# Modulation groups, branch A's keys and branch B's norm sums in a two-layer transformer block: three edits of order and layout

## The reference, cut to what matters

```python
def rms_norm(x, g):
    y = xf * lax.rsqrt(jnp.mean(xf * xf, axis=-1, keepdims=True) + NORM_EPS)
    return (y * g.astype(jnp.float32)).astype(x.dtype)
def modulate(h, shift, scale):
    return h * (1 + scale) + shift
...
mod_lat = (jax.nn.silu(c) @ w_ada[l] + b_ada[l])[:, None, :]
p_l = modulate(rms_norm(x, lp['g_norm1']), sh1, sc1) @ lp['w_in']
...
q, k, v = _split(p, (A_Q_W, A_KV_W, A_KV_W))          # branch A: 512 + 128 + 128 columns
q = rms_norm(q.reshape(b, t, A_HEADS, HEAD_DIM), q_gain)   # keys the same, then both rotated
...
cq, ckv, kr = _split(p, (B_Q_LORA, B_KV_LORA, B_ROPE))  # branch B: 384 + 256 + 32 columns
q = (rms_norm(cq, q_gain) @ w_q_up).reshape(b, t, B_HEADS, B_NOPE + B_ROPE)
kv = (rms_norm(ckv, kv_gain) @ w_kv_up).reshape(b, t, B_HEADS, B_NOPE + B_V)
```

## Time and profile before

| | us |
|---|---|
| median of 3 runs | 2586.5 |
| lowest and highest | 2586.43 and 2590.49 |
| profiled execution: its own time | 2591.72 |
| profiled execution: span of the records | 2589.9 |

### The profile page before, as it was taken

The page is one execution under the profiler, slowest core; times in us unless marked ns, Lnnn a source line. Parts: engine busy times, 40 slices in busy tenths (PEclk is TensorE's granted clock), DMA queues, the critical chain, the costliest instruction groups (busy, mean ns, idle before and its releaser), DMA issues. The chain is left out here.

```text
span 2589.9 us, 46521 instructions
## 1 busy us (share of the span) xinstructions
PE 2490.4 (96%) x20808; PEld 1476.5 (57%) x20808; DVE 805.2 (31%) x1651; ACT 574.8 (22%) x1233; POOL 233.7 (9%) x243
## 2 busy tenths in 40 slices
PE   6999999999999999999999999999999999999998
PEld 4444654455555554444444445556466667687887
DVE  2542333253444432121010002441555554321101
ACT  3353323122223211020000002441332323111100
POOL 0000000122222300000000000010022323000000
PEclk9999999999999999999999999999999899899999
DMA  7102111233232334222222224112122111145443
GB/s 285 50 17 73 42 57 49 90 105 110 67 139 68 132 111 151 73 98 81 74 75 79 73 81 151 49 66 90 41 83 67 51 59 60 61 138 177 154 155 106
DMA packets 64391, 238.81 MB, mean 92 GB/s; under 512 B 7009, under 2 KB 8049, under 8 KB 63425
## 3 DMA queue, kind: packets, MB, share of 16 engines
q1 hardware_dynamic: 61824, 220.23, 25.1%
...
HBM read 234.76 MB, written 1.05 MB: 91 GB/s over the span
## 5 line engine op out<-in xcount | busy, mean ns | idle before, releaser
L420 PE MATMUL psum<-normed,panel_ring 128*128 128x512 f32 (+1 forms) x3136 | 1166.4, 517 | 5.1 <-ACT normed L648 4.1
L420 PEld LDWEIGHTS psum<-normed,panel_ring 128*128 128x128 f32 x3136 | 575.6, 191 | 425.6 <-issue 374.0
L420 PE MATMUL psum<-arena,panel_ring 128*128 128x512 f32 (+1 forms) x1792 | 609.8, 494 | 1.8 <-ACT arena L1067 1.8
L420 PE MATMUL psum<-arena 64*64 64x64 f32 (+5 forms) x12696 | 522.0, 251 | 41.6 <-ACT arena L739 10.3
L420 PEld LDWEIGHTS psum<-arena 64*64 64x64 f32 (+2 forms) x12696 | 343.3, 141 | 334.1 <-issue 214.6
L420 PEld LDWEIGHTS psum<-arena,panel_ring 128*128 128x128 f32 x1792 | 335.2, 191 | 225.7 <-issue 200.3
L714 DVE TENSOR_REDUCE softmax_stats<-psum 128x1 f32<-128x512 f32 (+1 forms) x144 | 83.8, 600 | 178.8 <-PE psum L420 177.7
L739 ACT ACTIVATE arena<-psum,softmax_stats 128x512 f32<-128x512 f32 (+1 forms) x144 | 87.7, 613 | 220.0 <-PE psum L697 111.0
L1819 DVE TENSOR_TENSOR arena<-arena 128x512 f32<-128x512 f32 (+1 forms) x64 | 35.8, 559 | 305.8 <-ACT arena L1806 305.8
L1695 DVE SCALAR_TENSOR_TENSOR arena<-psum,modulation,arena 128x256 f32<-128x256 f32 x24 | 10.9, 480 | 313.9 <-PE psum L420 313.9
L1571 POOL TENSOR_SCALAR arena<-arena 128x64 f32<-128x64 f32 x96 | 72.2, 766 | 323.2 <-DVE arena L1617 178.1
...
## 6 DMA issues: line engine op xcount, KB each, us to landing
panel_ring<-panels SPq DMA_DIRECT2D x398, 512.0 KB, 3.3
arena<-panels SPq DMA_DIRECT2D x16, 512.0 KB, 14.8
...
```

The costliest lines, as they stand in the source:

```text
L420: return nc.tensor.matmul(out, lhsT, rhs, start=start, stop=stop, skip_group_check=check)
```

## The change

1. At the start, the sums of squares on TensorE come behind modulation group 0, and the spread of `stage_scale` comes behind group 1. `ROW3` gets a second bank (6).
2. Branch A projects the keys first. `begin` waits for the keys and the first query tile at group 0 and for one further query tile at each later group of heads.
3. Branch B sums squares with tokens on partitions. GpSimd adds the square tiles of a group (two additions for the queries, one for the keys and values), TensorE turns the result into two columns per 128 tokens, ScalarE takes the root of these few columns, VectorE their reciprocal, TensorE spreads them again, and ScalarE copies the spread tile out of PSUM. The key-value sums come ahead of the sixth panel, and the key part's rotation ahead of the second spread. Nine more steps of B are placed before A's attention: its third panel and the first sums. Bank counts and step counts follow.

```diff
                     e.wait_ge(x_in[k // 4].h, 16)
                 nc.scalar.activation(h[:, k, :], x[:, k, :], ACT.Square).then_inc(squared.h, 1)
             yield
+            yield
 
         def pe(e):
+            yield
             e.wait_ge(added.h, added.at(KT - 2))
             token_sums(bank, acc, T, True)
             e.wait_ge(squared.h, squared.at(KT))
@@ -595,7 +597,8 @@
                     e.wait_ge(added.h, added.at(k - 1))
                 nc.vector.tensor_tensor(acc, h[:, 0, :] if k == 1 else acc, h[:, k, :], ALU.add).then_inc(added.h, 1)
             yield
-        return Stage(name, 1, pe=pe, act=act, dve=dve)
+            yield
+        return Stage(name, 2, pe=pe, act=act, dve=dve)
 
 
     def stage_scale(name, l, tok, bank, sums_full, final=False):
...
         col0 = 0 if l < DEPTH - 1 else CTX
 
         def pe(e):
-            begin(e)
             for s in range(n_items + 3):
                 if s < n_items:
                     g, qt = items[s]
                     t, half, nk = groups[g]
+                    if qt == 0 and half == halves[0][0]:
+                        begin(e, t)
                     if exp_done.at(2 * (s - 1) + 2) > 0:
                         e.wait_ge(exp_done.h, exp_done.at(2 * (s - 1) + 2))
                     for i in range(2):
...
         qw = slice(0, T) if l < DEPTH - 1 else mid
         lat = slice(qw.stop - qw.start - SEQ, qw.stop - qw.start)
         q, k, v, rot, sq, tmp, consts = (at[n] for n in ("a_q", "a_k", "a_v", "a_rot", "a_sq", "a_tmp", "t_consts"))
-        tile = [q[:, j, :] for j in range(4)] + [k]
-        n_of = [qw.stop - qw.start] * 4 + [T]
+        tile = [k] + [q[:, j, :] for j in range(4)]
+        n_of = [T] + [qw.stop - qw.start] * 4
         proj, sums, rots, vb = (Banks("a_" + n, b, t) for n, b, t in
                                 (("proj", [0, 1, 2], 5), ("sums", [3], 5), ("rots", [4], 5), ("values", [5], 1)))
         squared, normed, rotated = sem("a_squared", 5), sem("a_normed", 5), sem("a_rotated", 5)
...
         def pe(e):
             for s in range(7):
                 if s < 5:
-                    for i, _ in enumerate(panel_fm(e, proj, l, P_A + s, h, qw if s < 4 else full_row, ready if s == 0 else None)):
+                    for i, _ in enumerate(panel_fm(e, proj, l, P_A + (s + 4) % 5, h, qw if s else full_row, ready if s == 0 else None)):
                         if i < 7:
                             yield
                 if s == 5:
...
                     e.wait_ge(sums.free.h, sums.free.at(j + 1))
                     r = tmp[:, j % 2, :n_of[j]]
                     link(e, nc.vector.reciprocal(r, r))
-                    gain = drv[:, l, 54:55] if j < 4 else vec[:, l, VEC["a_k"]:VEC["a_k"] + 1]
+                    gain = drv[:, l, 54:55] if j else vec[:, l, VEC["a_k"]:VEC["a_k"] + 1]
                     e.wait_ge(proj.free.h, proj.free.at(j + 1))
                     nc.vector.scalar_tensor_tensor(tile[j], tile[j], gain, r, ALU.mult, ALU.mult).then_inc(normed.h, 1)
                 if j >= 1:
...
                     nc.vector.tensor_tensor(t, t, turned, ALU.add).then_inc(rotated.h, 1)
                 yield
 
-        def begin(e):
-            e.wait_ge(rotated.h, rotated.at(5))
-            e.wait_ge(vb.free.h, vb.free.at(1))
+        def begin(e, t):
+            e.wait_ge(rotated.h, rotated.at(t + 2))
+            if t == 0:
+                e.wait_ge(vb.free.h, vb.free.at(1))
         return Stage(f"A{l}", 50, pe=pe, act=act, dve=dve, pool=pool), begin
 
 
...
-        b = Banks("proj", [6, 7], 25)
+        b = Banks("proj", [6, 7], 27)
         ups = (("nope", 0), ("rope", 0), ("nope", 1), ("turn", 0), ("rope", 1), ("nope", 2), ("turn", 1), ("nope", 3))
-        taken = {u: 9 + n for n, u in enumerate(ups)}
...
-            ("squared", 5), ("normed", 5), ("rotated", 3), ("k_filled", 1)))
+        squared, normed, rotated, k_filled, added, inverted = (sem("b_" + n, t) for n, t in (
+            ("squared", 5), ("normed", 5), ("rotated", 3), ("k_filled", 1), ("added", 3), ("inverted", 2)))
         width = [nq] * 3 + [T] * 3
 
         def pool(e):
             e.wait_ge(loadable[0].h, loadable[0].at(loadable[1]))
...
-            yield from idle(52)
+            yield from idle(15)
+            e.wait_ge(squared.h, squared.at(2))
+            nc.gpsimd.tensor_tensor(sq[:, 0, :nq], sq[:, 0, :nq], sq[:, 1, :nq], ALU.add).then_inc(added.h, 1)
+            yield from idle(8)
+            e.wait_ge(squared.h, squared.at(3))
+            e.wait_ge(added.h, added.at(1))
+            nc.gpsimd.tensor_tensor(sq[:, 0, :nq], sq[:, 0, :nq], sq[:, 2, :nq], ALU.add).then_inc(added.h, 1)
+            yield from idle(17)
+            e.wait_ge(squared.h, squared.at(5))
+            nc.gpsimd.tensor_tensor(sq[:, 3, :], sq[:, 3, :], sq[:, 4, :], ALU.add).then_inc(added.h, 1)
+            yield from idle(14)
             e.wait_ge(rotated.h, rotated.at(1))
             for hd in range(8):
                 p = nc.gpsimd.tensor_copy(k[64:96, hd, :], kr[64:96, :])
@@ -872,19 +887,40 @@
             yield from idle(15)
 
         def pe(e):
-            for g, (j0, n, _, _, nw) in enumerate(groups):
-                for j in range(3 * g, 3 * g + 3):
-                    yield from panel_fm(e, b, l, P_B + j, h, qw if j < 3 else full_row)
+            def sums(g):
+                j0, _, _, _, nw = groups[g]
                 ps = b.take(e)
-                for j in range(n):
-                    e.wait_ge(squared.h, squared.at(j0 + j + 1))
-                    p = mm(ps[:, :nw], ones, sq[:, j0 + j, :nw], j == 0, j == n - 1)
+                e.wait_ge(added.h, added.at(2 + g))
+                for tt in range(nw // P):
...
+
+            def spread_norm(g):
+                nw = groups[g][4]
+                ps = b.take(e)
+                e.wait_ge(inverted.h, inverted.at(g + 1))
+                for tt in range(nw // P):
+                    p = mm(ps[:, tt * P:(tt + 1) * P], rs[:, g, 2 * tt:2 * tt + 1].broadcast_to([P, P]), ident, True, True)
+                p.then_inc(b.full.h, 1)
+
+            for j in range(4):
+                yield from panel_fm(e, b, l, P_B + j, h, qw if j < 3 else full_row)
+                if j == 2:
+                    sums(0)
+                    yield
+            spread_norm(0)
+            yield
+            for j in range(4, 6):
+                yield from panel_fm(e, b, l, P_B + j, h, full_row)
+                if j == 4:
+                    sums(1)
+                    yield
             e.wait_ge(consts_t_in.h, consts_t_in.at(16 * (l + 1)))
-            e.wait_ge(b.free.h, b.free.at(7))
+            e.wait_ge(b.free.h, b.free.at(9))
             ps = b.take(e)
             mm(ps[:P, :SEQ], consts[64:96, T_PB:T_PB + P], kr[64:96, mid], True, True).then_inc(b.full.h, 1)
+            yield
+            spread_norm(1)
             yield
             e.wait_ge(small_b_in.h, small_b_in.at(16 * (l + 1)))
             e.wait_ge(normed.h, normed.at(3))
...
 
         def act(e):
-            for g, (_, _, wide, _, nw) in enumerate(groups):
-                for j in range(3 * g, 3 * g + 3):
-                    yield from idle(7)
-                    ps = b.arrived(e)
-                    if j < 5:
-                        nc.scalar.activation(sq[:, j, :width[j]], ps[:, :width[j]], ACT.Square).then_inc(squared.h, 1)
-                        nc.scalar.activation(lora[:, j, :width[j]], ps[:, :width[j]], ACT.Copy).then_inc(b.free.h, 1)
-                    else:
-                        nc.scalar.activation(kr[64:96, :], ps[64:96, :], ACT.Copy).then_inc(b.free.h, 1)
+            def root(g):
+                _, _, wide, _, nw = groups[g]
+                ps = b.arrived(e)
+                nc.scalar.activation(rs[:, g, :2 * nw // P], ps[:, :2 * nw // P], ACT.Sqrt, bias=eps, scale=1.0 / wide).then_inc(b.free.h, 1)
+
+            def keep(g):
+                nw = groups[g][4]
+                ps = b.arrived(e)
+                nc.scalar.activation(rs[:, g, :nw], ps[:, :nw], ACT.Copy).then_inc(b.free.h, 1)
+
+            for j in range(6):
+                yield from idle(7)
+                ps = b.arrived(e)
+                if j < 5:
+                    nc.scalar.activation(sq[:, j, :width[j]], ps[:, :width[j]], ACT.Square).then_inc(squared.h, 1)
+                    nc.scalar.activation(lora[:, j, :width[j]], ps[:, :width[j]], ACT.Copy).then_inc(b.free.h, 1)
+                else:
+                    nc.scalar.activation(kr[64:96, :], ps[64:96, :], ACT.Copy).then_inc(b.free.h, 1)
+                yield
+                if j in (2, 4):
+                    root((2, 4).index(j))
                     yield
-                ps = b.arrived(e)
-                nc.scalar.activation(rs[:, g, :nw], ps[:, :nw], ACT.Sqrt, bias=eps, scale=1.0 / wide).then_inc(b.free.h, 1)
-                yield
+                if j == 3:
+                    keep(0)
+                    yield
             ps = b.arrived(e)
```

(47 more changed lines are left out.)

9 lines of the change are left out of this document (6 added, 3 removed).

## The result

The changed kernel took 2571.9 us (median of five runs, 2569.5 to 2576.6) beside 2586.4 for the kernel before: a ratio of 0.9947, 95% interval 0.993 to 0.9965. The forecast was 2581.6 with a range down to 2575.5. The kernel gained about 13.7 us where 4.9 were expected. The profiled execution took 2576.6 us, with a span of 2574.8.

The account below looks back on a forecast made before the run. TensorE, busy 96% of the span, was taken as the bound; gains of -8.9 and -12.1, costs of +6.4 and +6.5, clock +3.2 and start 0 gave -4.9 us, from 2586.5 to 2581.6, range 2575.5 to 2588.

Parts of the forecast that it names:

- (l): Layer 1, A's last tiles: shorter reciprocal of key columns, -1.5 us; B's third panel covers the last rotation, -1.3.
- (b): Layer 0, A's attention: the 3.8 us wait queued on VectorE goes as its reciprocal shrinks to a few columns, -3.8.
- (h): Layer 0: VectorE's first scaling waits for ScalarE's copy of the spread tile and stands ahead of the maxima, +1.2 us.
- (f): Layer 0: B's first sums, behind the third panel, wait for ScalarE's square, GpSimd's addition and hand-overs, +2.1 us.
- (i): Layer 0: key-value sums, one matmul behind an attention step, wait for square, addition and hand-overs, +2.8 us.
- (q): Layer 1: B's first sums wait for square and addition, with tiles of 256 columns, +1.4 us.
- (r): Layer 1: VectorE's scaling stands ahead of the attention's maxima, +0.6 us.
- (s): Layer 1: key-value sums wait for square and addition, with two matmuls standing before them, +2.5 us.
- rival 2: In A and B, the new waits cost clock every time, four slow stretches instead of two: 2584.8 us; chance 0.17.
- rival 4: At the four waits for sums, GpSimd's additions are long, 2.88 us each: 6.3 more in all, 2587.9; chance 0.07.
- Rival 5: ScalarE's table switches carry a drain, 1.4 us in each layer: 2584.4 us; chance 0.04.
- (g): Layer 0: the root stands before the exponentials, so the table load begins only then and second scores come late, +0.3 us.

Follow-up runs that it names:

- a whole block: The kernel before plus 64 idle matmuls (256 TensorE instructions) at the start, nothing else: 2585.1 us, ratio 1.0005.
- before again: The kernel before, unchanged, profiled and timed once more: 2582.5 us, ratio 0.9985.
- cover: The changed kernel with branch B's sums one panel later and eight more steps of B ahead of A's attention: 2556.2 us, ratio 0.9881.
- half a block: The kernel before plus 32 idle matmuls (128 instructions) at the start: 2581.4 us, ratio 0.9982.

## Why the prediction was wrong

**The step that failed is the sum itself.** "-8.9 + 6.4 - 12.1 + 6.5 + 3.2 + 0" has terms for the start and for A and B in both layers and none for the rest: all behind them was taken as unchanged because its instructions were. The first paragraph said that a wait of TensorE or a slow stretch counts in full wherever it stands, and then looked for them only where the edits are. The wait of 1.50 at 928 and the 20.5 us at half clock behind 2205 lie in the profile before, in windows that I did not open.

**Where the gain came from.** All in mean values: at an equal time at the lower clock the changed kernel is 9.8 us faster (runs of both corrected by the slope), and it spends 6.8 us less there, 2.7 us by the slope: 12.5. (These are means over all runs; the 13.7 above is the ratio of the first five, 0.9947, put on 2586.4.) Of the 9.8, the windows corrected in the same way (two executions of each kernel) put 1.7 us on layer 0's A and B, 3.7 on layer 1's, 1.9 on the first scan, 0.9 on the second, 0.7 on the start, which sums to 8.9. Of the part for A and B the clock took back about 2 us: its time at the lower level there rose from a mean of 20.4 us to 25.6. So A and B together gave some 3.4 us and the start 0.7, together 4.1; the other 8 came from where nothing was edited: 2.8 in the scans, nearly 5 by less time at the lower clock outside A and B, and 0.9 that no window shows. The forecast of 4.9 for the edited stages lies near these 4.1, and that is in part luck: the terms without the clock came out 1.8 better than forecast and the clock 3.3 worse.

**Is it the place of the instructions?** Three things are shown by the runs. Where the waits for issue can stand is set by the number of the instruction modulo 256: 20 of 20. Shifting alone moves the time by as much as the change's outside gain: 20 idle matmuls in the kernel before gave 0.9961, and a whole block gave 1.0005. It moves the time at the lower clock too: 55.4 us with 80 instructions more and 50.8 with 128 more, but 67.2 with 256 more, beside 69.5 for the kernel before, with standard errors of 1.4 to 4.6. Undoing the shift in the changed kernel took its gain away, 0.9999, though 1.6 us at the start and a mean of 21.4 us more at the lower clock (8.6 by the slope) are in that, not only the 3.2 us of waits.

What the waits are for, the traces show as well. They hold each packet of queue q8 with its time. Put in order, the j-th packet belongs to instruction 194 + 256 j (the last packet has none in the program): in all 2299 pairs of the 14 traces TensorE came to that instruction 1.19 us or more after the packet's end, never sooner, and each of the 20 waits ended 1.23 to 1.60 us after the end of its packet. So these are waits for the fetch of the next block. Four of the pairs, in us:

| kernel | instruction | packet | TensorE before it |
|---|---|---|---|
| before | 18370 | 926.22 to 927.21 | stands from 927.01 to 928.50 |
| before again | 37058 | 2199.47 to 2200.42 | no wait, passes at 2203.41 |
| changed | 18370 | 921.30 to 922.45 | no wait, passes at 923.93 |
| cover | 18370 | 919.38 to 920.30 | stands from 919.49 to 921.78 |

The last two rows are the same number and the same matmul, the 16th of a group of 64. The packet started while TensorE was 227 instructions away in the one and when it had arrived in the other. So the number alone doesn't decide whether a wait comes; it comes where the packet starts late, and what sets its start is open. That fits the misses: half a block gave a time between the two ranges written down, and the kernel with cover got no faster with 12 idle matmuls.

What stays open is the clock. A stretch at the lower level, of 3.4 to 20.5 us, begins within 3 us of the end of 15 of the 20 waits, which is far from chance, as only 62 begin in the whole of the scans, some 14,000 us. But 5 waits have none behind them, the one at 928 in the kernel before among them, and 47 of the 62 stretches, such as the 13.7 us at 2023 in the changed kernel, stand behind no such wait. That the waits set off a part of the slow stretches is likely and not shown.

**Term by term.** Most steps in A and B held nearly to the tenth; the table has those that the trace shows as a wait of their own.

| term | predicted | measured |
|---|---|---|
| start | 0, modulation at 34.9 to 35.7 | 35.15; group 3's pass at 31.90 (32.1) |
| (a), (d) last rotation, evictions, layer 0 | -1.3, -1.7 | no such wait left |
| (l) last tiles and rotation, layer 1 | -1.5, -1.3 | no such wait left |
| (b) with (h), maxima | -3.8 + 1.2 | 3.79 became 0.57: -3.2 |
| (f) first sums, layer 0 | +2.1 | 2.12 |
| (i) second sums, layer 0 | +2.8 | 2.76 |
| (p) second panel's keys | +1.2 | 1.19 |
| (q) first sums, layer 1 | +1.4 | 1.37 |
| (r) maxima, layer 1 | +0.6 | no such wait |
| (s) second sums, layer 1 | +2.5 | 2.40 |
| (t) key part's rotation | +0.8 | 0.72 |
| clock in A and B | -1.6 - 2.9 + 3.2 = -1.3 | about +2 |

Leaving the clock out, the terms for the two layers sum to -0.9 and -2.7; measured are -1.7 and -3.7. Two sizes were off. (h) and (r) were too high by 0.6 each: the maxima hardly wait behind the scaling now. The clock was too low by some 3 us: each layer got a stretch of 6.8 us instead of 3.4, at 145.9 and 1661.4, right behind the waits for the second sums; the changed kernel's other profile has four stretches, one behind each new wait, of 6.8, 3.4, 3.4 and 6.8. In A and B that is rival 2. It is outside them that the clock turned.

At the start, the pass of group 0 was right (3.64 at 15.29), but group 1's 64 matmuls took 1.96 us and not 3.6, the sums 1.8 and not 3.5, and VectorE's passes ended at 30.0, not 33.6 to 34.5. It made no difference, because group 3's panel sets the time.

The additions took 1.26 us, near the row of 1.07 and far from 2.88, so rival 4 is out. Rival 5 is out as well. The load for the exponentials in layer 0, in ScalarE's timeline of the kernel after:

```profile
110.03 0.27 ACT L957 ACTIVATE arena<-psum,const_global 128x8 f32<-128x8 f32 x1 [2.06 <-PE psum L420]
110.31 1.28 ACT L743 ACT_TABLE_LOAD   x1
111.61 0.47 ACT L743 ACTIVATE arena<-psum,softmax_stats 128x256 f32<-128x256 f32 x1
```

The load follows the root by 0.01 us, and the exponential the load by 0.02. The drain that the Trainium skill gives ("ScalarE: Activation LUTs", section What ACT_TABLE_LOAD costs) is not to be seen here; term (g) stands at the load alone.

**The baseline.** The profile of before was an execution with 84.2 us at the lower clock, where its runs have 69.5 on average; 14.7 us more are 5.9 by the slope. Its own time lay 5.2 above the median, and the prediction took that off as a whole without asking what it was.
